# Twelve turns of expert tiles moved from the early up products into the first three pairs of heads of the delta rule

## What is computed

```
xn   = rmsnorm(x, mix_norm_w);  proj = xn @ w_in
y_a  = pool_mixer(...) @ w_pool_up
y_b  = deltanet_branch(qkv, z, ...) @ w_dn_up        # 8 heads, gated delta rule
h    = x + (sigmoid(gate_a) * y_a + sigmoid(gate_b) * y_b) @ w_mix_out
q    = rmsnorm(h) @ w_query                          # peer_ffn: 16384 experts, 8 heads x top 16
u    = take(expert_down, experts);  act = gelu(h . u)
h    = h + (gates * act) . take(expert_up, experts)
```

## Time and profile before

| | |
|---|---|
| median of 3 runs | 2876.53 us (2875.24 to 2883.41) |
| the profiled execution | 2882.74 us |
| its span | 2881.0 us |
| busy: TensorE, VectorE, ScalarE, GpSimd | 93%, 66%, 39%, 30% |
| TensorE's granted clock, mean | 0.97 |
| DMA, mean | 198 GB/s |

### The profile page before, as it was taken

One profiled execution on the slowest core, in us unless ns is written; L12 is line 12 of the kernel. 1 busy time (PEld: TensorE's weight loads), 2 busy tenths in 40 slices (PEclk: granted clock), 3 DMA queues, 4 the chain that ended last, 5 costly groups with the idle time before them and its releaser, 6 DMA issues. The chain is left out here.

```text
span 2881.0 us, 39144 instructions
## 1 busy us (share of the span) xinstructions
PE 2692.9 (93%) x13559; PEld 2267.0 (79%) x13559; DVE 1898.0 (66%) x3324; ACT 1112.5 (39%) x1670; POOL 876.4 (30%) x768
## 2 busy tenths in 40 slices
PE   7998888999899988989999999999979999998998
PEld 5677777687789887778999999999957767766887
DVE  5785554565698896767777877877845763454334
ACT  4443324323235775333333333333343333454222
POOL 1002344200146775014444545554410230033000
PEclk9999999999999999999999999999989999999999
DMA  4766554397383445999999989999822112201332
GB/s 157 229 204 205 184 163 152 105 317 238 132 248 126 169 169 192 368 337 368 313 317 311 323 296 319 316 314 316 284 73 88 52 44 81 74 1 52 95 95 88
DMA packets 250560, 569.90 MB, mean 198 GB/s; under 512 B 23600, under 2 KB 138416, under 8 KB 248752
## 3 DMA queue, kind: packets, MB, share of 16 engines
q1 hardware_dynamic: 208400, 406.72, 42.6%
q0 software_dynamic: 36864, 134.23, 13.2%
q10 hardware_dynamic: 5152, 27.11, 2.4%
HBM read 468.89 MB, written 99.09 MB: 197 GB/s over the span
## 5 line engine op out<-in xcount | busy, mean ns | idle before, releaser
L230 DVE TENSOR_TENSOR split<-raw,split 128x1024 fp32r<-128x1024 f32 x368 | 450.2, 1224 | 514.1 <-ACT split L221 513.9
L221 ACT ACTIVATE split<-raw 128x1024 fp32r<-128x1024 f32 x424 | 447.5, 1056 | 772.6 <-PE up L1572 207.1
L1570 PE MATMUL up<-split,weight_high 128*128 128x512 f32 x768 | 302.6, 394 | 19.8 <-DVE weight_low L2546 13.2
L1571 PE MATMUL up<-split,weight_high 128*128 128x512 f32 x768 | 303.4, 395 | 0.0
L1572 PE MATMUL up<-split,weight_low 128*128 128x512 f32 x768 | 303.2, 395 | 0.0
L1845 POOL DMA_INDIRECT picked_rows<-down_rows,picked x128 | 186.0, 1453 | 316.7 <-DVE picked_rows L2555 172.7
L1845 POOL DMA_INDIRECT picked_rows<-in_stream,picked x128 | 204.0, 1594 | 207.2 <-DVE acc L2564 181.6
L272 DVE STREAM_TRANSPOSE turn<-turn 128x1024 f32<-128x1024 f32 x128 | 158.0, 1237 | 95.4 <-DMA down_rows<-turn 47.8
L1570 PEld LDWEIGHTS up<-split,weight_high 128*128 128x128 f32 x768 | 146.0, 190 | 51.8 <-issue 23.6
L1572 PEld LDWEIGHTS up<-split,weight_low 128*128 128x128 f32 x768 | 145.8, 190 | 31.0
L230 POOL TENSOR_TENSOR split<-raw,split 128x1024 fp32r<-128x1024 f32 x56 | 139.5, 2490 | 97.1 <-ACT split L221 97.1
(11 more groups left out here) (522 smaller groups left out, 6498.2 us busy)
## 6 DMA issues: line engine op xcount, KB each, us to landing
raw<-in_stream SPq DMA_DIRECT2D x440, 512.0 KB, 5.3
turn<-in_stream SPq DMA_DIRECT2D x128, 512.0 KB, 5.4
down_rows<-turn SPq DMA_DIRECT2D x512, 128.0 KB, 4.3
gates<-stage ACTq DMA_DIRECT2D x12, 2048.0 KB, 7.3
gate<-gates SPq DMA_DIRECT2D x30, 768.0 KB, 8.6
h<-in_x SPq DMA_DIRECT2D x4, 512.0 KB, 5.9
h<-in_x SPq DMA_DIRECT2D x1, 2048.0 KB, 8.7
h_saved<-h SPq DMA_DIRECT2D x1, 2048.0 KB, 7.6
```

Source lines behind the costliest of these rows:

```text
L221: act.activation(g.high[t % slots], g.raw[:, t % RAW, :], ACT.Copy).then_inc(g.high_split, 1)
L230: dve.tensor_tensor(g.low[t % slots], g.raw[:, t % RAW, :], g.high[t % slots], ALU.subtract).then_inc(g.low_split, 1)
L1570: pe.matmul(bank, xh, hi[:, w], start=start, stop=False, skip_group_check=True)
L1571: pe.matmul(bank, xh, lo[:, w], start=False, stop=False, skip_group_check=True)
```

## The change

```diff
-TURN_CONV, TURN_DELTA, TURN_MERGE, TURN_QUERY, TURN_EARLY = 22, (12, 12, 12, 8), 22, 16, 24
+TURN_CONV, TURN_DELTA, TURN_MERGE, TURN_QUERY, TURN_EARLY = 22, (16, 16, 16, 8), 22, 16, 12
```

## The result

| | before | after |
|---|---|---|
| median | 2878.6 us (2875.2 to 2883.4, 4 runs) | 2924.3 us (2918.4 to 2933.0, 4 runs) |
| ratio, 95% interval | | 1.016 [1.013, 1.019] |
| the profiled execution, its span | 2882.7 us, 2881.0 us | 2918.4 us, 2916.4 us |

The kernel became 45.7 us slower by the medians. The profiled executions are only 35.7 us apart: the one of before lies near the upper end of its runs, and the one of after is the fastest of its four.

What follows compares the result with a forecast made beforehand. The prediction took VectorE's turns and their DMAs to bound the first three pairs' levels. Terms +68 (delta rule), +3 (clock) and -16 (early products) gave +55 us on 2876.5, so 2932 us; range 2910 to 2953 us.

Steps and rivals of the forecast that it cites:

- The bound: First three pairs' delta rule levels: VectorE's turns and their DMAs set the path, 45.0 us in the first pair.
- The gain: Early up products: twelve turns leave, the stage ends at 1272.6 in place of 1289.5; 16 us saved.
- The cost: Delta rule, first three pairs: four added turns each cost 22.7 us a pair, 68 us in all.
- my walk: Turn-by-turn timing of a pair's six levels from load and store waits: 44.8 us with 12 turns, 67.5 with 16.
- round trips: Levels of the first three pairs: turns wait 5.3 us for a load, 6.8 us for a level's first store.
- a rate limit: Rival in the levels: rings at a rate limit, added turns at 4.0 us each, +32 us, 2908 us; chance 0.13.
- The rival's price: Rival in the levels: added turns keep the present pace of 4.0 us each, 2908 us; chance 0.13.
- The clock: Behind the first three pairs' levels: TensorE's lower granted clock adds 1 us a pair, 3 us in all (0 to 12).
- The other side: Rival in the levels: added turns fill VectorE's idle time, break-even 1.3 us each; chance 0.03 faster, 0.03 same.
- The walk with the shorter durations: A pair's levels with the skill page's DMA times (3.2 us for 512 KB): 37 us before, 58 after, 21 more.

Runs made afterwards that it cites:

- the delta part alone: Changed kernel's 16 turns in each of the first three pairs, but the early up products keep the kernel before's 24; 2938.9 us, ratio 1.020 to the kernel before.
- the mended order: Each turn stored right behind its load: on the changed kernel (16 turns) 2895.6 us, on the kernel before (12 turns) 2868.9 us.

## Why the prediction was right, and where it was off

**The bound, and the direction.** The reading that VectorE's queue, by way of the turns, already set the end of the first three pairs held: the added turns found no cover, the fourth pair stayed at 38.9 us, and VectorE's waits for TensorE stayed at 1.0 us. 2924 us lies in the range and 8 us below the forecast of 2932. By the trace the forecast is further off: the two stretches gave +41.6 us, where the sum had +55. The mechanism was right, its cost too high.

**The gain.** 16 us forecast, 15.7 us in the trace, 14.6 us by the medians of the run with the delta part alone. Its working held in its parts: the stage took 129.4 us against "about 129", the first dot lost its wait, and TensorE became the bound.

**The cost, the mis-sized term.** Forecast 22.7 us a pair and 68 us in all; measured 18.0 to 19.4 us a pair, 56.2 us. The places of the waits came out as walked: a load wait ahead of each third turn, a store wait ahead of the first turns of levels 3 and 6. By levels, the forecast was 4.8, 11.8, 14.5, 10.3, 11.6 and 14.5 us; the first pair has 4.7, 11.6, 15.2, 8.7, 11.1 and 13.1.

Three things make up the difference. The first is a slip in my walk: by its own rules turn 12 starts at 45.6 + 5.3 = 50.9 us and not at 51.8, which gives 66.6 us of levels and 21.8 us a pair. The second is the store trip taken from two-turn levels: I put 6.8 us from the end of every level. In the trace of after it is 5.7, 5.8 and 5.5 us behind levels of three turns (245.66 to 251.33, 260.83 to 266.66, 280.65 to 286.12). It is 7.5 us behind level 4 with its two (269.51 to 277.01), which delayed nothing, since the turn that follows waited for its load even so. And the second store of level 3 let its turn go 1.6 us after the first one's, where I had 2.3. The third goes the other way: the load of the third turn of level 3 came 7.0 us behind the turn before it in the same buffer (252.58 to 259.58), where I had 5.3. SP wasn't free for it:

```profile
246.06 6.76 SPq L285 DMA_DIRECT2D down_rows<-turn  x12
252.93 0.38 SPq L706 DMA_DIRECT2D raw<-in_stream  x1
253.35 7.83 SPq L265 DMA_DIRECT2D turn<-in_stream  x3
```

It was busy with twelve store issues and a filler's load until 253.3 us. My walk let loads go out at once, with no queue ahead of them. Why the store trip is shorter behind three turns isn't shown; that a lighter load of the rings shortens it is, by the runs with quarter loads, and behind three turns the first load has landed when the stores are issued.

**A reason that was only half right.** I argued round trips against a rate limit and gave the rate 0.13. The runs show that trips aren't all: order and third buffer together take 11 us off the 64.4 at full bytes, 8.6 of them by the order alone, and then 16 turns stay at 53 us, 3.3 us a turn, and come down to 45.8 us only with fewer bytes. That the rate of the engines is what holds the 53 us is argued from their share and not shown, since SP's queue is nearly full there too. The rival's price, 4.0 us a turn, missed too, since 4.7 us was measured. "Against: the third load can't be issued before the first turn is done" was no argument against a second limit close behind.

**The clock.** 3 us were forecast for the stretches behind the levels. The three pairs grew by 57.3 - 56.2 = 1.1 us outside of their levels, with the clock at 0.76 behind the first one. It fell in the levels themselves, where the waits hid it. The bound that I gave was too low: 9.6 us of busy TensorE at 0.84 are 16.1 us at half the clock, 6.5 us more and not 4.

**The other side.** No added turn was free. The cheapest added ones with full loads, in the mended order, cost 13.4 / 4 = 3.4 us each, 2.5 times the 1.3 us at which the change would have broken even.

**A side sum.** The walk with the shorter durations that the prediction tries beside the traced ones doesn't give 58 us for a pair after. By its own rules it gives 37 us before and some 53 us after, 16 us more and not 21, so the difference does depend on the durations. The forecast went by the traced ones.

## What to carry to other kernels

When work is moved into a chain, price it by what it does to the queues it brings, not by its own time: a turn of 1.2 us cost 4.7 us, since its load and its store had to go round between two uses of a buffer. When the stores of a group are issued behind its last step, even the group's first buffer comes free late; issuing each store as soon as its data is there was worth 29 us here with 16 turns and 11 us with 12, for one line. And once an order is mended, look at what else is nearly full before adding buffers, the DMA engines and the queue that issues to them alike: with 16 turns a third input buffer turned load waits into store waits and took 2.7 us off a pair's levels, with 12 turns 4.1 us.

## What the runs showed of the hardware that I had not expected

The time from issue to landing of the same DMA depends on what else is on the rings: 128 KB stores land in 3.7 us (median) beside full loads and in 2.4 to 2.5 us beside quarter loads, and the store trip differed by 2 us between levels of two and of three turns in one trace.

Issuing has a price of its own: twelve stores kept SP's queue for 6.76 us in the changed kernel, 0.56 us each, and a load that was due had to wait behind them.

TensorE's granted clock moves times in stretches that a change doesn't touch. The stretch from the heads' roots (L1382) to the first product of the next stage is the same work in all kernels; before, and with stores behind their loads and 12 turns:

```profile
522.30:567.50 45.20, 41.08 (x138) 25.48 (x139) 28.53 (x35) 16.15 (x23) 0.00 (x0) 0.96 0.20 68
...
513.60:565.80 52.20, 48.08 (x138) 28.67 (x139) 28.53 (x35) 16.27 (x23) 0.00 (x0) 0.80 0.20 66
```

The second is 7 us longer with the clock at 0.80, and 10 us longer with 0.75 in the run with 16 turns. The changed kernel takes 45.3 us there, at 0.96. The two kernels with the long stretch also had the widest spreads, 24 and 27 us over ten runs each, and the one profiled was the slowest of its ten both times. With stores behind their loads and 16 turns, the mean clock of a whole run goes from 0.972 in the fastest (2883.1 us) to 0.961 in the slowest (2910.5 us). In this stretch VectorE and TensorE alternate in small steps, and the traces don't show what makes the clock fall in one execution and not in the other; that stays open.
